# Merging the sample tokens in two groups of 256 instead of one of 512, in a hybrid trunk-and-expert kernel

## What is computed

```python
ga, gb, gc = jnp.split(jax.nn.sigmoid(pg), N_BRANCH, axis=-1)
merged = ga * (ya @ wb[0]) + gb * (yb @ wb[1]) + gc * (yc @ wb[2])
x = x + g1 * (merged @ lp['w_out'])
h = rms_norm(x, lp['norm2']) * (1 + sc2) + sh2
# peer_ffn, for each block hb of 128 tokens, 8 heads, 128 keys in each of two lists:
q = (hb @ lp['p_wq']).reshape(P_BLOCK, P_HEADS, 2, P_KEY_DIM // 2)
s1, s2 = q[:, :, 0] . p_key1,  q[:, :, 1] . p_key2
# top 16 of each list, top 16 of their 256 sums -> 16 experts for each head, softmax gate
act = jax.nn.gelu(jnp.einsum('td,thkd->thk', hb, u_tab[expert]))
y   = jnp.einsum('thk,thkd->td', gate * act, v_tab[expert])
```

## Time and profile before

| | us |
|---|---|
| median of 3 runs | 3300.24 |
| lowest, highest | 3297.59, 3304.46 |
| span of the profiled execution | 3309.6 |
| PE busy | 2778.2 (84%) |
| DVE busy | 1856.9 (56%) |
| ACT busy | 902.0 (27%) |
| POOL busy | 903.8 (27%) |
| bytes moved | 801.75 MB, of them 671.13 MB by the gathers |

### The profile page before, as it was taken

How to read it: one execution, slowest core, us unless ns; L and a number is a source line. 1 busy time by engine, 2 the same in 40 slices (tenths; PEclk the granted TensorE clock), 3 DMA queues, 4 the chain that set the end, 5 groups by cost and what they waited for, 6 DMA issues and landing times.

```text
span 3309.6 us, 44601 instructions
## 1 busy us (share of the span) xinstructions
PE 2778.2 (84%) x15826; PEld 1573.3 (48%) x15826; DVE 1856.9 (56%) x3915; ACT 902.0 (27%) x2333; POOL 903.8 (27%) x812
## 2 busy tenths in 40 slices
PE   6989989898999999888789977777777777777776
PEld 4756665676666666765333433322332233222322
DVE  1028977544333433234667578787667667765454
ACT  2113333004221222122223322333323332332233
POOL 0000000000000000000233345555555555555553
PEclk8999997999999999889899999999999999999999
DMA  5112230211111111055789899999999999999997
GB/s 205 60 36 86 99 107 15 91 56 48 33 33 33 33 33 33 16 205 225 269 332 381 330 385 405 420 417 420 408 416 417 421 404 421 420 415 416 420 419 308
DMA packets 139480, 801.75 MB, mean 242 GB/s; under 512 B 15560, under 2 KB 26568, under 8 KB 53929
## 3 DMA queue, kind: packets, MB, share of 16 engines
q0 software_dynamic: 92160, 671.13, 49.4%
q1 hardware_dynamic: 47144, 128.24, 11.2%
HBM read 785.42 MB, written 13.89 MB: 242 GB/s over the span
## 4 chain that ended last, share of the span: by engine, by line
DMA 25%; PE 12%; DVE 6%; issue 5%; ACT 3%; POOL 2%; POOLq 0%; ACTq 0%; DVEq 0%; SPq 0%; PEldq 0%
DMA pr_rows<-in_p_uv,pr_now 23%; PE pr_psy L2613 7%; DVE pr_rows L2941 4%; POOL pr_rows L2502 2%; PE pr_pss L2578 2%; PE pr_pss L2564 1%; PE pr_pss L2556 1%; DMA early<-in_w_branch 1%; ACT pr_diag L2716 1%; DMA early<-gate_scratch 1%; ACT pr_weight L2699 1%; ACT pr_act L2709 0%; DVE pr_acc L2953 0%; PE pr_pss L2571 0%; DVE pr_top_i L2858 0%
## 5 line engine op out<-in xcount | busy, mean ns | idle before, releaser
L2613 PE MATMUL pr_psy<-pr_rows,pr_diag 128*128 128x512 f32 x2432 | 1149.1, 620 | 349.6 <-ACT pr_diag L2716 338.1
L2502 POOL DMA_INDIRECT pr_rows<-in_p_uv,pr_now x640 | 808.4, 1263 | 880.1 <-PE pr_psy L2613 768.6
L2613 PEld LDWEIGHTS pr_psy<-pr_rows,pr_diag 128*128 128x128 f32 x2432 | 454.9, 196 | 1032.3 <-issue 602.2
L2941 DVE CUSTOM_DVE_ANT_0 pr_rows<-pr_rows,h_tok 128x1024 f32<-128x1024 f32 x376 | 457.9, 1225 | 317.4 <-DMA pr_rows<-in_p_uv,pr_now 313.6
L2941 DVE CUSTOM_DVE_ANT_0 pr_rows<-pr_rows,pr_part 128x1024 f32<-128x1024 f32 x256 | 311.9, 1226 | 150.4 <-DMA pr_rows<-in_p_uv,pr_now 146.5
L1872 POOL TENSOR_TENSOR yT<-rw_sys,rw_bmask 128x128 f32<-128x128 f32 x40 | 18.1, 454 | 1328.4 <-DVE rw_sys L1971 1328.4
L2709 ACT ACTIVATE pr_act<-pr_dot 128x2 f32<-128x2 f32 x316 | 64.1, 203 | 1065.9 <-DVEq L2947 1065.8
L1376 PE MATMUL rw_gate_ps<-hT,rw_gate_w 128*128 128x320 f32 x768 | 277.1, 484 | 2.8 <-ACT rw_gate L1365 2.8
L2716 ACT ACTIVATE pr_diag<-con,pr_weight 128x128 f32<-128x128 f32 x632 | 217.5, 391 | 0.4 <-ACT pr_weight L2699 0.2
L1376 PEld LDWEIGHTS rw_gate_ps<-hT,rw_gate_w 128*128 128x128 f32 x768 | 137.5, 200 | 60.6 <-issue 20.4
L2699 ACT ACTIVATE pr_weight<-pr_gate,pr_act 128x1 f32 (+1 forms) x640 | 153.6, 286 | 29.2 <-ACT pr_act L2709 1.6
(11 more groups left out here) (440 smaller groups left out, 3373.7 us busy)
## 6 DMA issues: line engine op xcount, KB each, us to landing
hg_ada_w<-in_w_ada SPq DMA_DIRECT2D x16, 1024.0 KB, 5.2
rw_gate_w<-in_w_in SPq DMA_DIRECT2D x24, 512.0 KB, 4.1
pr_rows<-in_p_uv,pr_now POOLq DMA_INDIRECT x640, 12.4
st_ada_w<-in_w_ada SPq DMA_DIRECT2D x4, 2048.0 KB, 17.3
hg_w<-in_w_in SPq DMA_DIRECT2D x16, 512.0 KB, 3.7
rw_w<-in_w_in SPq DMA_DIRECT2D x15, 512.0 KB, 3.6
gate_scratch<-rw_gate SPq DMA_DIRECT2D x24, 320.0 KB, 4.2
mg_w<-in_w_branch SPq DMA_DIRECT2D x12, 512.0 KB, 9.0
```

Of the source, the lines that this page charges most:

```text
L2502: nc.gpsimd.indirect_dma_start(out=rows[:, r].rearrange("p u d -> p (u d)"), out_offset=None, in_=A["p_uv"], in_offset=bass.IndirectOffset ...
L2613: last = nc.tensor.matmul(ps_y[:, c % 2, a], diag[:, r], rows[:, r, 1, a * 512:(a + 1) * 512], start=(first and r == 0), stop=False, skip_ ...
L2941: nc.vector.tensor_tensor_reduce(out=rows[:, r, 0], in0=rows[:, r, 0], in1=h_tok[c % 2], scale=1.0, scalar=0.0, op0=ALU.mult, op1=ALU.add, ...
```

## The change

The sample tokens are merged in two groups of 256. Group 0 is merged in chunk 0, group 1 in chunk 1 and the first turns of chunk 2. Each group loads all weight tiles (12 of `w_branch`, 8 of `w_out`, 8 of `p_wq`); gates are loaded for 256 columns, in a ring of 8. Eight branches of group 0 come before turn 0. `AFTER` becomes `TASKS`, by chunk and turn; the banks are handed out by a list of all users, and are counted afresh after each `scores`. Some buffers get memory of their own (`h_tok1`, `rstd`, `rstd_f`; `sq_f` now lies in `acc`). The routing windows move to fit.

```diff
+GROUPS, GW, GRING = 2, 2 * P, 8
+LOADS = PAIRS + 2 * KD
-        EARLY = 12
-        AFTER = {t: [("branch", i) for i in range(EARLY + 4 * t, EARLY + 4 * t + 4)] for t in range(3)}
-        AFTER.update({3 + t: [("out", 2 * t), ("out", 2 * t + 1)] for t in range(4)})
-        AFTER[7] = [("sums", 0)]
-        AFTER.update({8 + t: [("q", 2 * t), ("q", 2 * t + 1)] for t in range(4)})
-        AFTER[12] = [("tok", 1), ("scores", 1)]
+        EARLY = 8
+        BRANCHES = 3 * KD
+        TASKS = {(0, 0): [("branch", i) for i in range(EARLY, EARLY + 6)],
+                 (0, 1): [("branch", i) for i in range(EARLY + 6, EARLY + 11)],
+                 (0, 2): [("branch", i) for i in range(EARLY + 11, BRANCHES)],
+                 (0, 3): [("out", i) for i in range(3)], (0, 4): [("out", i) for i in range(3, 6)],
+                 (0, 5): [("out", i) for i in range(6, KD)], (0, 6): [("sums", 0)],
+                 (0, 8): [("q", i) for i in range(3)], (0, 9): [("q", i) for i in range(3, 6)],
+                 (0, 10): [("q", i) for i in range(6, KD)], (0, 11): [("tok", 1), ("scores", 1)]}
+        TASKS.update({(1, t): [("branch", BRANCHES + i) for i in range(3 * t, 3 * t + 3)] for t in range(8)})
+        TASKS[1, 5] = [("scores", 2)] + TASKS[1, 5]
+        TASKS[1, 2] = TASKS[1, 2] + [("tok", 2)]
+        TASKS.update({(1, 8 + t): [("out", KD + i) for i in range(2 * t, 2 * t + 2)] for t in range(4)})
+        TASKS[1, 12] = [("sums", 1)]
+        TASKS.update({(1 + (14 + t) // TURNS, (14 + t) % TURNS): [("q", KD + i) for i in range(2 * t, 2 * t + 2)]
+                      for t in range(4)})
+        TASKS[2, 2] = [("scores", 3)]
+        def before(task):
+            n = USERS.index(task)
...
+            back = since(n)
+            return [USERS[n - 4] if back >= 4 else USERS[n - back - 1]]
...
+                def gate(i):
+                    g, m = divmod(i, BRANCHES)
+                    sp.wait_ge(br_taken, i - GRING + 1)
+                    sp.dma_start(mg[:, i % GRING], A["gate_scratch"][m][:, tokens(g)]).then_inc(g_in[i % GRING], 16)
+                for g in range(GROUPS):
+                    for m in range(LOADS):
+                        if LOADS * g + m >= RINGW:
+                            weights(LOADS * g + m)
+                        if RINGW <= m < PAIRS:
+                            gate(BRANCHES * g + 2 * m)
+                            gate(BRANCHES * g + 2 * m + 1)
+                        elif g == 0 and m >= LOADS - RINGW:
+                            gate(BRANCHES + 2 * (m - LOADS + RINGW))
+                            gate(BRANCHES + 2 * (m - LOADS + RINGW) + 1)
...
-                        if i == 13:
+                        if i == 12:
                             take_tok(1)
                             take(1)
...
+                for i in range(TURNS):
+                    def between(i=i):
...
+                        if i == 6:
+                            take(2)
+                    turn(1, i, between=between)
+                    follow(1, i)
...
-                soon, routes[1] = routes[1][:6], routes[1][6:]
+                soon, routes[1] = routes[1][:EARLY // 2], routes[1][EARLY // 2:]
-                ROUTING = {0: [(1, 0, 4), (2, 4, 20), (3, 20, 36), (4, 54, 62)],
-                           1: [(5, 0, 12), (6, 12, 28), (7, 28, 60)], 2: [(8, 6, 60)], 3: [(9, 6, 60)]}
+                ROUTING = {0: [(1, 0, 4), (2, 4, 20), (3, 20, 36), (4, 50, 62)],
+                           1: [(5, 0, 10), (6, 10, 22), (7, 26, 60)], 2: [(8, 14, 60)], 3: [(9, 6, 60)]}
```

More of the change, by code:

```diff
@@ new lines, in peer_stage @@
+        TASKS[2, 2] = [("scores", 3)]
+        BY_VECTOR = (2, 6)
+        USERS = [("scores", 0)] + [("branch", i) for i in range(EARLY)] + [
+            task for at in sorted(TASKS) for task in TASKS[at] if task[0] != "tok"] + [("scores", 4)]
+        since = lambda n: n - max(m for m in range(n) if USERS[m][0] == "scores") - 1
+        BANK = {task: since(n) % 4 for n, task in enumerate(USERS) if task[0] != "scores"}
+        def before(task):
+            n = USERS.index(task)
+            if task[0] == "scores":
+                last = {}
+                for what, i in USERS[max(n - 4, 0):n]:
+                    last[what] = max(i, last.get(what, 0))
+                return list(last.items())
+            back = since(n)
+            return [USERS[n - 4] if back >= 4 else USERS[n - back - 1]]
@@ L2451, in peer_stage, with tokens, own @@
+        def tile(what, i):
+            return tiles[:, BANK[what, i], 0:GW]
+        def tokens(g):
+            return slice(LP + GW * g, LP + GW * g + GW)
+        def own(g):
+            return slice(GW * g, GW * g + GW)
         with nc.Block() as block:
@@ L2468, in weights @@
-                    ins.then_inc(w_in[n % RINGW], 16)
[L2470 to L2476, removed]
+                    g, m = divmod(n - RINGW, LOADS)
+                    if m < PAIRS:
+                        sp.wait_ge(br_mm, BRANCHES * g + 2 * m + 2)
+                    elif m < PAIRS + KD:
+                        sp.wait_ge(out_mm, KD * g + m - PAIRS + 1)
+                    else:
+                        sp.wait_ge(q_mm, KD * g + m - PAIRS - KD + 1)
@@ L2529, in weights, with free @@
                         pe.wait_ge(w_in[n % RINGW], 16 * (n // RINGW))
[L2531 to L2543, removed]
+                def free(task):
+                    for what, i in before(task):
+                        if what == "scores":
+                            pe.wait_ge(s_taken, i + 1)
+                        elif what == "branch":
+                            pe.wait_ge(br_taken, i + 1)
+                        elif what == "out":
+                            pe.wait_ge(out_taken, i + 1)
+                        elif what == "sums":
+                            pe.wait_ge(log_done, i + 1)
+                        else:
+                            pe.wait_ge(q_taken, i + 1)
                 def transposes(c, src, done):
@@ L2551, in task @@
                     if what == "branch":
-                        m, b = MERGE_ORDER[i]
-                        weights(i // 2)
-                        free(what, i)
+                        g, j = divmod(i, BRANCHES)
+                        m, b = MERGE_ORDER[j]
+                        n = LOADS * g + j // 2
+                        weights(n)
+                        free((what, i))
                         for k in range(KW):
-                            last = nc.tensor.matmul(tile(what, i), wpair(i // 2)[:, i % 2, k], K.yT[b][:, k, LP:T],
+                            last = nc.tensor.matmul(tile(what, i), wpair(n)[:, j % 2, k], K.yT[b][:, k, tokens(g)],
                                                     start=(k == 0), stop=(k == KW - 1))
@@ L2777, in _ @@
+                    for what, x in TASKS.get((c, i), []):
+                        if what == "sums":
+                            act.wait_ge(sum_done, x + 1)
+                            rsqrt_log(K, rstd[:], tile("sums", x), 1.0 / D, "rms").then_inc(log_done, 1)
+                            act.wait_ge(log_done, x + 1)
+                            rsqrt_exp(K, rstd[:]).then_inc(root_done, 1)
                 take(0)
@@ L2836, in _ @@
                     final_squares(c - 1)
-                    turns(c, 3, 10)
+                    turn(c, 3, between=(lambda: take(c + 1)) if c == 2 else None)
+                    turns(c, 4, 10)
                     final_root(c - 1)
```

191 lines of the change are left out of this document (100 added, 91 removed).

## The result

| | before | after |
|---|---|---|
| median, us (14 runs of each) | 3303.76 | 3317.68 |
| lowest, highest | 3295.6, 3315.25 | 3302.94, 3332.03 |
| ratio, 95% interval | | 1.0044 (1.0028 to 1.0059) |
| span of the profiled execution | 3309.6 | 3318.4 |
| first gather to last row landed | 1744.3 | 1757.3 |

What follows compares the result with a forecast made beforehand. DMA was taken to bound chunks 1 to 4, with 78.6 us unfilled in chunk 0. Winning 36 us there against 36.5 of loads and waits of 7 and 3 gave +12.7, 3313 us (forecast 3307 to 3323; 8 in 10: 3287 to 3332).

Steps and rivals of the forecast that it cites:

- Loads: Chunks 0 to 2: loading weights twice adds 28 loads, 36.4 us of DMA time, with no fixed cost on top.
- The start: Start of chunk 0: eight early branches finish sooner, so turn 1's gathers go out near 1565 us, 31 us earlier.
- The stops: Chunk 0, turns 1 to 3: TensorE held at a branch for a PSUM bank, DMA drains, 37.8 us a period.
- The first rival: Chunk 0: the bank stops open no gaps, turns 1 to 3 take 25 us each; 3275 us, chance 0.10.
- The rest of chunk 0: From turn 5 DMA is full and the stops around the root go; chunk 1's first gather 36 us earlier, at 1954.
- Chunk 1's stop: Turn 6 of chunk 1: three branches behind scores(2) wait for banks until ScalarE's copy; 7 us lost.
- Other small waits: Chunk 1: all other waits of the three engines on each other cost 3 us, between 0 and 16.
- the third rival: Chunk 1: VectorE's work above DMA's in early turns loses 24 us more; 3337 us, chance 0.14.
- Behind chunk 1: From chunk 2's first gather on, only the last q tasks differ, costing under 1 us.
- The second rival: Stops are there but 3 to 6 us cheaper each, chunk 1's stop absorbed; 3293 to 3301 us, chance 0.21.
- the fourth: The rival that each of the 28 loads adds an unhidden fixed 1.9 us; 3366 us, chance 0.03.

Runs made afterwards that it cites:

- run a: Changed kernel with twelve early branches instead of eight and four branches after each of turns 0 to 2; 3277.52 us, 0.993 of the kernel before.
- b: Changed kernel keeping eight early branches, with four after each of turns 0 to 3 and later tasks one turn later; 3279.49 us, 0.9948 of the kernel before.
- run g: Run e plus outs given 3, 3, 2 after three turns, leaving a turn without tasks after sums; 3284.29 us, 0.9953 of the kernel before.
- run d: Changed kernel without group 1's 28 weight loads, so its output is wrong; 3293.22 us, 0.9967 of the kernel before.
- run j: Run d plus wider chunk 1 routing windows (part 5 over 12 batches, part 6 over 13); 3283.25 us, 0.9945 of the kernel before.
- run e: Kernel before, one group, weights loaded once, with its gate ring grown from 4 to 8 tiles; 3279.42 us, 0.9921 of the kernel before.
- run f: Changed kernel with run a's task order and, in chunk 1, scores without branches behind them; 3267.63 us, 0.9896 of the kernel before.
- h: Run f with the token transposes put ahead of the branches after turn 2 of chunk 1; 3271.05 us, 0.9915 of the kernel before.
- i: Run f with wider chunk 1 routing windows (part 5 over 12 batches, part 6 over 13); 3270.18 us, 0.9885 of the kernel before.

## Why the prediction was right

It was right in sign and size: +12.7 us put, +13.0 in length, +13.9 between the medians. The stops and chunk 0 came out of the right mechanism. That the total came out so close is partly luck, as two errors of nearly 10 us cancel in it (see "Loads" below). So is the 3313: it took over the 9.4 us between span and median, which were 0.7 in the result, and a median of three runs that lay 3.5 us under that of 14.

- **The start.** Put: turn 1's gathers 19.3 us after the first one. Measured 18.5. VectorE's first product began 9.7 us after the first gather, put 10.3.
- **The stops.** Put: held branches before turns 2, 3 and 4, a period of 37.8 us, gathers 64, 102, 140 and 161 us after the first. Measured 64.9, 100.9, 138.4 and 159.1, with periods of 36.0 and 37.5. The sum's terms hold one by one. In turn 2: from the first gather to the last row landed 25.2 us (put 26.3, with the loads), from there to the held branch 4.1 (put 5.0), the branch 3.75 (put 4.6), to the next turn's first gather 2.9 (put 1.9). The stop over 10 us is 14.7 to 16.2. The held branch took its 3.75 us for 8 records, where the full clock needs 1.77 (32 in 7.07): 2.0 us for the clock, which had fallen while TensorE stood (granted 0.76 to 0.81 in these stretches, a mix of 1.2 and 2.4 GHz), put as 2.9. The DMA share of 0.68 to 0.78 was put as 0.6 to 0.8. Runs a and b show the cause: with four tasks a turn the stops are gone and 37 us with them. The first rival's time (3275) is that of run a, 3277.5: its mechanism is what the kernel would do without the banks' stops.
- **The rest of chunk 0.** Chunk 1's first gather 407.8 us after the first; put 408.3. The free turn behind `sums` was worth 10 us in the kernel with one group (run g).
- **Loads.** Put: 36.4 us. The DMA time is there, 28 tiles of 0.5 MB in `q1`. But their net price is 24.5 to 27 us, because a part of it falls into time that the other engines would leave open anyway. This is the term that was mis-sized, by 9.5 us. Without the loads the sum gives 12.7 - 36.4 = -23.7 us; run d measured -13.9 in length (1730.4 against 1744.3). So everything but the loads cost 9.8 us more than put, most of it in chunk 1.
- **Chunk 1's stop.** Put 7 us, measured 6.2 in its turn and 4 to 5 net.
- **Other small waits.** Put 3 us in chunk 1, from a range of 0 to 16. Of its 370.1 us 354.2 are transfer by the sum (321.6 for the gathers, 27.3 for the 21 loads whose packets lie in it, 5.3 for the gates), 6 are the scores' stop, and 10 are left. Without the loads 14 are left (run d): 4 us of such waits lie under the loads. The sum came out because it booked the loads in full and most of these waits not at all: chunk 1, gather to gather, took 366.0 us and 368 was put. So the third rival's mechanism was there (VectorE above DMA in early turns, shown by run j for 1.7 us), its 24 us weren't. What makes up the rest of these waits stays open.
- **Behind chunk 1.** "Under 1 us" was put. Chunk 2 took 327.1 us instead of 324.5, and without loads 324.0. It is small; three of the loads fall there, 3.9 us, which the sum had booked with chunk 1. At chunk 2's first gather the change stood at +10.0 us, put +12.7.
- **Slips in the working.** Chunk 1's 321.9 us run to 2312.0, while chunk 2's first gather is at 2309.55: from gather to gather it is 319.4. The sum sets its own 321.6 against that, and so holds 2.2 us that nothing in the change costs. The gate called a 256-column one at 0.65 us is the one of 256 KB, with 512 columns. The fixed cost of a transfer stands in the section of the Trainium skill's page DMA: Bandwidth & Descriptors that is named under run d, not in the section Bandwidth.

The second rival (cheaper stops) and the fourth (fixed cost of loads, 3366) fell. What decided the sum is then: 36 us won in chunk 0, where 37 more were lost to an order of tasks that doesn't fit the banks, and 47 given back in chunk 1.

## What to carry to other kernels

When one engine fills a ring of PSUM banks and another empties it only behind its own work of the next turn, hand out no more tasks in a turn than there are banks. One or two too many cost 12 us a turn here (37.2 over three turns), and the mend was another order of the same tasks. Before loading weights twice to spread work, ask what the first half of the change brings alone: the larger gate ring gave 26 us in the old kernel with no load more (run e), the two groups with all their loads, well ordered, about 3 us beyond that by length (run f against e, 1715.7 against 1718.5), which is hardly more than these lengths repeat. The medians of the two lie 11.8 us apart (3267.6 and 3279.4), with intervals that overlap (0.9861 to 0.9931 and 0.9898 to 0.9945), so the size of this last gain stays open. And price what makes room for a slack as carefully as the slack itself.

## What of the hardware was not expected

- Loads of 512 KB beside a stream of gathers (DMA share 0.98 over chunk 1) cost less than their own share of DMA: 26.9 us for 28, 0.96 us each, against 1.30 by their packets' time, since some fall into gaps that are there anyway. No fixed time on top was seen.
- VectorE at half the columns: line 3084 took 0.41 to 0.42 us for 256 where 512 took 0.68. The estimate was right, so the takes of 24 branches cost VectorE some 24 x 0.16 = 3.8 us more in two halves than in one piece.
- The stages ahead of the experts, nearly the same in all these kernels, ended up to 13 us apart from one profiled execution to the next (first gather from 1532.5 to 1545.7 us). So differences of single spans are worth little here. Lengths from the first gather repeat better: chunk 0 took 373.2, 372.8, 373.7 and 375.3 us in runs a, f, h and i, which are alike up to there.
